# Order of the sample path and of the state products in a hybrid decoder step

## What is computed

```python
h = rmsnorm(x) * (1 + scale1) + shift1
q, k, v, iq, ik, iw, z, xbc, dt, g_att, g_ssm = split(h @ w_in)
att = sparse_attend(...)             # prompt: causal top-k; samples: eight cached pages each
# SSD branch of the prompt, per chunk of 128 tokens and per head
y_diag = einsum(C B^T, decay, x*dt)  # inside the chunk
y_off  = einsum(C, state, exp(cs))   # from the state that enters the chunk
state  = state * exp(cs[-1]) + einsum(B, decay_end, x*dt)
y = group_rmsnorm((y_diag + y_off + d_skip*x) * silu(z))
# samples: one step of the same recurrence on eight states of 128 x 1024
merged = sigmoid(g_att)*att + sigmoid(g_ssm)*y
x = x + gate1 * (merged @ w_out)
x = x + gate2 * (relu(h2 @ w_up)**2 @ w_down)
```

## Time and profile before

| | us |
|---|---|
| device time, median of 3 runs | 2477.02 (2474.79 to 2477.5) |
| device time of the profiled execution | 2478.8 |
| its span, first to last instruction | 2477.0 |
| TensorE busy | 2234.4 |
| VectorE busy | 1467.5 |
| GpSimd busy | 834.0 |
| ScalarE busy | 611.1 |

### The profile page before, as it was taken

How to read it: one execution, slowest core, us unless ns; L and a number is a source line. 1 busy time by engine, 2 the same in 40 slices (tenths; PEclk the granted TensorE clock), 3 DMA queues, 4 the chain that set the end, 5 groups by cost and what they waited for, 6 DMA issues and landing times.

```text
span 2477.0 us, 33916 instructions
## 1 busy us (share of the span) xinstructions
PE 2234.4 (90%) x13159; PEld 2007.5 (81%) x13159; DVE 1467.5 (59%) x2413; ACT 611.1 (25%) x1009; POOL 834.0 (34%) x728
## 2 busy tenths in 40 slices
PE   7897999999999957774798999699999999999995
PEld 3893459999999947664577874299999999999994
DVE  1733335899999976775789875355333233232337
ACT  2202321110113332223567771122110110100103
POOL 0210024333333315431655541431424234234235
PEclk9897999999999978887899998899999999999997
DMA  6113422222222122243322007422101101101022
GB/s 269 55 58 120 153 68 102 94 85 94 102 81 89 77 89 60 70 102 58 88 49 44 26 1 259 166 103 86 52 35 51 51 34 68 34 34 68 34 94 77
DMA packets 111411, 203.21 MB, mean 82 GB/s; under 512 B 11445, under 2 KB 79045, under 8 KB 99781
## 3 DMA queue, kind: packets, MB, share of 16 engines
q1 hardware_dynamic: 95650, 163.90, 20.5%
q10 hardware_dynamic: 15670, 38.19, 4.1%
HBM read 161.06 MB, written 41.13 MB: 82 GB/s over the span
## 4 chain that ended last, share of the span: by engine, by line
PE 41%; DVE 4%; POOL 3%; issue 2%; ACT 2%; DMA 1%; SPq 1%; ACTq 0%; DVEq 0%; POOLq 0%
PE pj L1925 32%; PE px L1328 4%; PE pj L1317 2%; DVE Pr L1452 1%; PE pj L1568 1%; ACT PT L1381 1%; POOL q_hl L1251 1%; POOL OC L1917 0%; POOL wlo L1882 0%; PE pj L1305 0%; PE pj L1304 0%; DVE m8b L1438 0%; PE pj L1530 0%; DVE M L1415 0%; POOL Pr L1260 0%
## 5 line engine op out<-in xcount | busy, mean ns | idle before, releaser
L240 PE MATMUL pj<-act_hi,whi 128*128 128x344 f32 x1344 | 431.4, 321 | 3.5 <-POOL wlo L223 2.4
L240 PE MATMUL pj<-act_hi,wlo 128*128 128x344 f32 x1344 | 430.5, 320 | 0.0
L240 PE MATMUL pj<-act_lo,whi 128*128 128x344 f32 x1344 | 430.2, 320 | 0.0
L215 POOL CAST whi<-raw 128x512 fp32r<-128x512 f32 (+2 forms) x100 | 66.7, 692 | 628.6 <-PE pj L240 403.4
L1925 PE MATMUL pj<-ahi,whi 128*128 128x344 f32 x816 | 263.6, 323 | 2.1 <-DVE alo L2117 1.0
L1925 PE MATMUL pj<-ahi,wlo 128*128 128x344 f32 x816 | 261.8, 321 | 0.0
L1925 PE MATMUL pj<-alo,whi 128*128 128x344 f32 x816 | 261.4, 320 | 0.0
L240 PEld LDWEIGHTS pj<-act_hi,whi 128*128 128x128 f32 x1344 | 253.5, 189 | 3.8 <-issue 2.6
L240 PEld LDWEIGHTS pj<-act_hi,wlo 128*128 128x128 f32 x1344 | 253.5, 189 | 0.0
L240 PEld LDWEIGHTS pj<-act_lo,whi 128*128 128x128 f32 x1344 | 253.0, 188 | 0.0
L1925 PE MATMUL pj<-u_lo,d_hi 128*128 128x344 f32 x720 | 230.9, 321 | 0.0
(11 more groups left out here) (384 smaller groups left out, 4574.6 us busy)
## 6 DMA issues: line engine op xcount, KB each, us to landing
raw<-in_w_in SPq DMA_DIRECT2D x29, 1024.0 KB, 4.8
raw<-in_w_ada SPq DMA_DIRECT2D x24, 1024.0 KB, 4.8
raw<-in_w_up SPq DMA_DIRECT2D x16, 1024.0 KB, 4.8
raw<-in_w_down SPq DMA_DIRECT2D x16, 1024.0 KB, 4.8
scr_g<-O ACTq DMA_DIRECT2D x16, 516.0 KB, 2.7
scr_c<-E ACTq DMA_DIRECT2D x16, 516.0 KB, 2.7
xb<-scr_c SPq DMA_DIRECT2D x8, 1024.0 KB, 6.2
qt<-scr_q SPq DMA_DIRECT2D x32, 256.0 KB, 5.3
```

The source lines that it names most:

```text
L215: ins = pool.tensor_copy(whi[:, hs, 0:kt, c0:c1], a)
L240: ins = pe.matmul(pj[:, hs, n, 0:W3], w[:, hs, k], a[:, k, c], start=(k == 0 and m == 0), stop=(k == kt - 1 and m == 2))
```

## The change

In the SSD scan the state products are issued in two halves, each behind the values of groups 0 and 1, and VectorE multiplies each half with exp(cs) behind the normalisation and behind the gate. The scaling of the state moves ahead of the wait for the last values. The products of the state update come directly behind the last values.

In the sample path SyncE fetches the first two blocks of the output weights ahead of the pages of sample 6. VectorE normalises the last group and gates group 2 ahead of the state of sample 7. The last two subtractions for `alo` go from GpSimd to VectorE, behind that state. In `out_splits` the wait for the stored states moves from the third block to the fourth, with a wait for VectorE's last read of the states added.

```diff
@@ pe_ssd
+            def from_state(s, j):
+                for g in (2 * j, 2 * j + 1):
+                    ins = pe.matmul(pjf[0][:, g * 256:g * 256 + 256], xb[:, s, 12 + g], ST[:, g * 256:g * 256 + 256],
+                                    start=True, stop=True)
+                ins.then_inc(SD["yo"], 1)
+            def to_state(at, later):
+                ...
+                for g in range(4):
+                    ins = pe.matmul(pxf[:, g * 256:g * 256 + 256], Bn[:, g], xw[...],
+                                    start=True, stop=True)
+                ins.then_inc(SD["dst"], 1)
...
-                for g in range(4):
-                    ins = pe.matmul(pjf[0][...], xb[:, s, 12 + g], ST[...], start=True, stop=True)
-                ins.then_inc(SD["yo"], 1)
-                ...
+                    if g in (1, 2):
+                        from_state(s, g - 1)
+                    if g == 4:
+                        to_state(at, later)
@@ dve_ssd
                     if g == 2 and later:
                         gate(at, 1 - s)
+                    if g in (1, 2):
+                        j = g - 1
+                        dve.wait_ge(SD["yo"], at(2, g))
+                        if g == 1 and later:
+                            dve.wait_ge(SD["yt"], at(1, 0))
+                        link(dve.tensor_tensor(in_blocks(yn, j), by_head(pjf[0], j), ex[...], ALU.mult))
                 steps(1 - s, bass.ds(i * 2 + (s + 1), 1))
-                dve.wait_ge(SD["yo"], at(1, 1))
+                st3 = ST.rearrange("p (h d) -> p h d", d=64)
+                link(dve.tensor_tensor(st3, st3, ex[:, 32:48]..., ALU.mult))
                 dve.wait_ge(SD["y"], at(4, 4))
-                for j in range(2):
-                    ...
@@ sp_smp
             for b in range(1, NB):
+                if b == 6:
+                    sp_out(sp, (0, 1))
                 far_pages(sp, b, SP_PAGES)
@@ pool_smp
             low(2)
             low(3)
-            pool.wait_ge(SA["pt"], NB // 2)
-            pool.wait_ge(s_s1[2], 16 * len(range(2, NB, 3)))
-            low(0)
-            low(1)
@@ dve_smp
                 state(2 * g)
                 largest(g)
-                state(2 * g + 1)
+                if g < NB // 2 - 1:
+                    state(2 * g + 1)
                 normal(g)
                 if g:
                     gated(g - 1)
+            state(NB - 1)
+            dve.wait_ge(SA["pt"], NB // 2)
+            dve.wait_ge(s_s1[2], 16 * len(range(2, NB, 3)))
+            for k in range(2):
+                dve.wait_ge(s_mh, KT - 3 + k)
+                dve.tensor_tensor(alo[:, k, 0:T], M[:, k, 0:T], ahi[:, k, 0:T].bitcast(F32), ALU.subtract).then_inc(s_ml, 1)
@@ out_splits
             if n == 1:
                 pool.wait_ge(SA["ft"], NB // 2)
-                for x in range(3):
-                    pool.wait_ge(s_s1[x], 16 * len(range(x, NB, 3)))
...
+                if m == 3:
+                    pool.wait_ge(SS["y"], KT * NB)
+                    for x in range(3):
+                        pool.wait_ge(s_s1[x], 16 * len(range(x, NB, 3)))
@@ block.sync
             sp_smp(sp)
-            sp_out(sp, (0, 1))
             sp_x(sp)
```

More of the change, by code:

```diff
@@ L975, in squares @@
                     ins.then_inc(SD["ss"], 1)
+            def from_state(s, j):
[4 more added lines that the diff above has]
+            def to_state(at, later):
+                pe.wait_ge(SD["xw"], at(1, 1))
+                pe.wait_ge(SD["ex"], at(1, 1))
+                if later:
+                    pe.wait_ge(SD["rt"], at(1, 0))
+                for g in range(4):
+                    ins = pe.matmul(pxf[:, g * 256:g * 256 + 256], Bn[:, g], xw[:, 4 * g:4 * g + 4].rearrange("p h d -> p (h d)"),
+                                    start=True, stop=True)
+                ins.then_inc(SD["dst"], 1)
             def chunk(at, s, i, first, later):
@@ L1022, in chunk @@
                         ins.then_inc(SD["y"], 1)
-                for g in range(4):
-                    ins = pe.matmul(pjf[0][:, g * 256:g * 256 + 256], xb[:, s, 12 + g], ST[:, g * 256:g * 256 + 256],
-                                    start=True, stop=True)
-                ins.then_inc(SD["yo"], 1)
[L1029 to L1036, removed]
+                    if g in (1, 2):
+                        from_state(s, g - 1)
+                    if g == 4:
+                        to_state(at, later)
                 pe.wait_ge(SD["yn"], at(1, 1))
@@ L1164, in chunk @@
                         gate(at, 1 - s)
+                    if g in (1, 2):
[3 more added lines that the diff above has]
+                            dve.wait_ge(SD["yt"], at(1, 0))
+                        link(dve.tensor_tensor(in_blocks(yn, j), by_head(pjf[0], j),
+                                               ex[:, 8 * j:8 * j + 8].rearrange("p (u a) -> p u a", u=2).unsqueeze(3).broadcast_to([P, 2, 4, 64]),
+                                               ALU.mult))
                 steps(1 - s, bass.ds(i * 2 + (s + 1), 1))
-                dve.wait_ge(SD["yo"], at(1, 1))
+                st3 = ST.rearrange("p (h d) -> p h d", d=64)
+                link(dve.tensor_tensor(st3, st3, ex[:, 32:48].unsqueeze(2).broadcast_to([P, 16, 64]), ALU.mult))
                 dve.wait_ge(SD["y"], at(4, 4))
-                for j in range(2):
[L1170 to L1173, removed]
                 link(dve.tensor_tensor(in_blocks(yn, 0), in_blocks(yn, 0), by_head(pjf[1], 0), ALU.add))
                 dve.tensor_tensor(in_blocks(yn, 1), in_blocks(yn, 1), by_head(pjf[1], 1), ALU.add).then_inc(SD["yn"], 1)
-                st3 = ST.rearrange("p (h d) -> p h d", d=64)
-                link(dve.tensor_tensor(st3, st3, ex[:, 32:48].unsqueeze(2).broadcast_to([P, 16, 64]), ALU.mult))
                 dve.wait_ge(SD["yt"], at(1, 1))
```

## The result

| | before | after |
|---|---|---|
| device time, median of 6 runs each | 2477.26 (2473.51 to 2479.34) | 2458.58 (2451.68 to 2462.54) |
| ratio, 95% interval | | 0.9924 (0.9913 to 0.9936) |
| span of the profiled execution | 2477.0 | 2457.2 |
| TensorE's mean granted clock | 0.947 | 0.950 |

A forecast was written before the change was run, and what follows sets the result against it. Bound by VectorE's wait for late state products in the scan, loads nearly level, and by late output weights in the sample path. Scan 10.0 (2.6 + 6 x 0.8 + 2.6) plus samples 11.6 gives 21.6: 2477.0 to 2455.4 us, range 2443 to 2467.

The forecast's parts named there:

- the load chain: Scan, six middle chunks: gate ends at 15.8 us, third load sets the next start, 26.55 us a chunk, gain about 0.8 each.
- The tail of a chunk: Scan, from fourth ML to L1180: ends at 23.9 to 25.1 us instead of 27.2, gain 2.1 to 3.3, taken as 2.6.
- The last chunk: Scan, final chunk: nothing is loaded behind it, so it keeps the tail's whole gain of 2.6 us.
- half clock early in a chunk: Scan, sign that the forecast is wrong: a TensorE clock of 0.50 early in the chunks.
- the slower rival: Scan: TensorE stays at half clock, up to 7 us more a chunk, 2514 at worst; chance 0.07 with any other loss.
- The sample path: Weights fetched sooner and last group first: values of sample 6 start at 1587.4 against 1598.98, gain 11.6 us, bounds 7 and 14.5.
- The turn of the last group: Sample path, sign that the forecast is right: TensorE's turn at about 1583 less the scan's gain, its values 3 to 4 us later.
- The values of sample 6: Sample path: start at 1587.4 behind ScalarE's four casts (3.9 us), store of state 7 and copy of the probabilities.
- the part of the half clock left to the range: Sample path: a shorter wait may remove some half clock from the values of sample 6, 0 to 2.9 us, outside the sum.
- The displaced pages: Sample path rival: 2 MB of weights push pages of sample 6, state 5 and pages of sample 7 up to 5 us; 2460.4, chance 0.08.
- The sum's lower bound: Scan: least total gain 2.8 us, with six middle chunks losing 0.4 each; upper bound 15.6.
- its two ends: Scan: the first and the last chunk, which alone keep the tail's 2.6 us each.

The follow-up runs named there:

- The weights alone: Kernel before with only the earlier fetch of the output weights, ahead of the pages of sample 6: 2468.91 us, ratio 0.9959.
- the split kernel: Changed kernel with a chunk's first two loads issued once their buffer is free, only the gate values' load behind the gate: 2449.79 us, ratio 0.9892.
- the scan alone: Kernel before with only the change's scan part, sample path as before: 2468.53 us, ratio 0.9960.
- the constants: Twelve unread products on constants in TensorE's wait ahead of the fourth values: 2455.09 us added to the changed kernel, 2436.55 us added with split loads.
- the two other kernels with that code: Kernels with the sample path of before: the change's scan part only, 2468.53 us, and the kernel before with split loads, 2475.88 us.

## Why the prediction was right

**What bounds the kernel.** Right in both stages. The split of the loads shows that the load chain takes over as forecast (8.8 us in the changed kernel, nothing in the kernel before). The weights alone show that the last group waited for weights that it doesn't need.

**The tail of a chunk** was put at 23.9 to 25.1 us, the two ends standing for the state's products at 1.89 and 3.11 us. With the loads out of the way it is 24.8 (short chunks) and 26.4 (long ones) in the split kernel, and 23.4 at full clock. So at full clock the sum was right within 0.5 us. At half clock the state's products take 3.73 us rather than 3.11, and the last values and the transposes are longer as well, which the bound did not count: the 3.11 us of the earlier trace rows begin at 1080.37, and the half clock ends at 1082.70. Chunk 0 gained 2.9 us (2.6 forecast).

**The load chain** was right through two errors that cancel. The gate was to be held up by GpSimd's scaling until 14.7 us and to end at 15.8, and a chunk to follow 10.75 behind it, 26.55 in all. The gate is held up as said and ends 1.1 us behind the scaling. But the scaling ends at 15.0 us in chunk 4, which begins at full clock (the product ahead of it takes 2.42 us instead of 1.90), and at up to 16.1 in chunks 2 to 6, the latest where the chunk begins at half clock. So the gate ends at 16.1 to 17.2 us there (19.3 in chunk 7). The loads land 9.7 to 10.6 us behind it (median 7.2 us after the third issue, 8.0 before). The five steps from chunk 2 take 26.8 us on average, against 27.5 before. That this is so near to 26.55 is partly luck, as the same scan code took 27.8 in the profile of the scan alone. Chunk 1 gained 2.6, not 0.8: its gate ends at 13.9 us, so the loads are in 23.7 us after its start, 0.8 us behind VectorE's release.

**The last chunk** is the step that failed: -2.6 forecast, +1.7 measured. The tail was taken at the clock that the trace of before showed. In the trace of after, the chunk starts behind a wait of 2.95 us for its load, runs its first 9.4 us at half clock and takes 3.73 us for its state's products. In the profile of the scan alone it takes 46.16 us, nothing gained and nothing lost. With the loads split it takes 43.48 us, -2.7 against before, and with the constants, loads still late, 42.75. So the size of the tail's gain was right, and the clock took it. The prediction had half clock early in a chunk as a sign of the slower rival; it came in mild form, in some chunks, at some 4 us in the last one, and the mean clock from chunk 2 to chunk 7 fell from 0.88 to 0.84.

**The sample path** went as forecast, 12.3 against 11.6, but some 2 us of the 12.3 come from the trace of before: the two other kernels with that code take 119.45 and 119.75 us there instead of 121.76. The weights landed 46.3 and 48.8 us after the first scores, ahead of the pages, and GpSimd split them from 1551.64 us on. The turn of the last group stands at 1577.62; 1583 less the 6.9 us by which this stage now starts sooner is 1576. The values of sample 6 stand at 1581.73 behind ScalarE's casts of 3.79 us (3.9 forecast), against 1587.4 - 6.9 = 1580.5. They took 5.72 us instead of 6.55, the part of the half clock left to the range. The displaced pages cost nothing in this profile: TensorE waits 1.09 us for the last ones, 1.34 before. That was luck in part. The prediction took 7.6 us for the 2 MB, the time of the first of the two loads; both took 10.1 us before and 10.9 here. It looked for the loss at the pages of sample 7, while in half of the profiles with early weights TensorE waits for those of sample 5, and in three of them some 4 us are lost. What the prediction did not separate is that the order on VectorE and the two subtractions have no share in this that the runs can tell.

**The sum's lower bound.** The 2.8 us given for the scan take 2.6 us for its two ends, where the tail's own lower value is 2.1; with it the bound is 1.8, and 2468 for the whole instead of 2467. The measured time lies far from either.

**What stays open.** The constants show what the half clock costs, and the variants show that moving a wait moves the clock's fall. Why the fall lasts 3.4 us in one chunk and 6.8 in the next, with the same wait of 3.2 us ahead, wasn't settled. It also wasn't tried to copy the probabilities on ScalarE ahead of its casts, which are now the last wait of the sample path.

## What to carry to other kernels

When a serial chain is shortened, look for what else hangs on its middle: here the loads hung on the gate, and about half of what the scan could gain appeared only when two of the three were taken off it. A short wait of TensorE can cost twice, in itself (3.2 us here) and in the clock of the work behind it (1.4 to 3.0 us). So a wait that can't be removed may be worth filling, and a move that turns one wait into three can lose more than it saves. When two engines contend for a stretch, moving one instruction out of it may put the next one in: price the whole queue. And a load that is moved forward can delay what it meets on the way, which a single profile may not show.

## What the runs showed of the hardware

Twelve products whose result nobody reads, 2.90 us of TensorE's time a chunk, made the kernel 13.2 us faster: the granted clock between chunks 2 and 7 was 1.00 with them and 0.89 without (99.08 of 129.30 us busy in the split kernel). The instructions behind were 1.7 to 1.9 times as fast: the state's products 1.95 against 3.73 us, the transposes 1.09 against 1.87.

VectorE's multiplication of 128x1024 by 128x1024 took 1.21 to 1.22 us alone and 2.91 beside a GpSimd multiplication, and the normalisation 1.51 against 4.68 to 4.72. GpSimd's scaling took 2.34 us whether it met the one or the other.
